# Summing the second router's modulation inside the time mix, and filling the spare expert rows at the start

## The chip, the cores and the metric

The kernel runs on one core of a Trainium2 chip. A core has five engines that follow their own instruction streams and meet at semaphores: TensorE (PE, matrix products), VectorE (DVE), ScalarE (ACT), GpSimd (POOL) and SyncE (SP, which here only issues transfers). The time is device microseconds of one launch of the whole program; the figure of a kernel is the median of its runs.

## The reference

It is a network of two layers on 512 tokens of width 1024, all in float32. What matters here is how the modulation vectors enter:

```python
c_act = jax.nn.silu(c)
for layer in range(2):
    shift, scale, gate = _ada(c_act, ada_w[layer, 0], ada_b[layer, 0])   # c_act @ w + b, split in 3
    h = _rmsnorm(x) * (1 + scale) + shift
    y = even_mixer(h) if layer == 0 else rwkv7_time_mix(h)
    x = x + gate * y
    shift, scale, gate = _ada(c_act, ada_w[layer, 1], ada_b[layer, 1])
    h = _rmsnorm(x) * (1 + scale) + shift
    x = x + gate * moe(h)                # router, two of 16 experts for each token
return _rmsnorm(x) * final_norm_g
```

Each of the four modulations is one vector of 1024 times a 1024 x 3072 matrix, which is 12 MB of weights. They depend on c alone, so they can be worked out anywhere ahead of their use. The last of the four (index 3 in the kernel) belongs to the mixture of experts of layer 1 and is first needed there. The time mix computes three wide projections (v, r and k, each 1024 x 1024) and several narrow ones (w, a, g) of six mixtures of the tokens with their predecessors, and then a recurrence.

## The kernel before

The program is one block with a stream for each engine, in this order of stages: the front (load x, norm, modulation 0), the five projections of layer 0 (q, k, v, u, z), attention and spatial gating, the output product (`out_proj(0, 5)`) with the router's logits in it, the routing and the experts of layer 0 (`moe(0)`), the time mix (`rwkv()`: projections, scan, output product) and the experts of layer 1 (`moe(1)`). Every order is written out by hand. PSUM banks are handed out by `bank_plan`, which lists the uses in PE's order; six banks rotate in ring "a", and the use of a bank waits until the one six places before it is drained.

**A modulation** takes three steps. SP loads 24 pieces of 512 KB (`ada(L, m)` of the sync stream, L610) into a ring of four buffers, `aring`; the load of a piece waits until DVE is done with the piece four before it. DVE multiplies each piece with its column of c and adds it to `acc` (L1205 for the first of a third, L1207 for the rest), one 128x1024 operation for a piece. Then PE sums over the partitions: `mod(k)` is 24 matmuls with a 128x128 block of `acc` as the weights and a single column of ones (L1698). The trace records each float32 matmul as two, so this is "x48". Last, DVE adds the bias (L1213, L1217). `mod(0)` and `mod(1)` make modulation 0 (16 and 8 matmuls), and `mod(2)`, `mod(3)`, `mod(4)` make modulations 1, 2 and 3. Where they stand: `mod(2)` between the products u and z, `mod(3)` at the end of attention, `mod(4)` at the start of `moe(0)`, ahead of the product that ranks the tokens (L1873, L1876).

**The ranking product** waits for "chosen", which DVE signals in `route` at L413 after a chain of small operations. DVE's part of `mod(4)` stands later in `route`, ahead of its wait for that product (L427).

**The 24 pieces of modulation 3** are worked on by DVE in layer 0's output product: 8 ahead of `router_weights(0)` and 4 after each of the first four tiles of `residual(0)`. `aring` and `acc` lie in areas 6 and 7 of the arena. The same areas hold `CB`, the gathered expert rows of `moe`, until all sixteen tiles of x are updated ("x_done" 16), and later R1 and K1 of the time mix.

**The expert rows.** The experts write their rows by item into `expert_rows` (`y_dram`) in DRAM, 24 blocks of 128 rows, of which 16 to 24 are used. SP fills the last eight blocks once with finite numbers: 4 MB from areas 3 and 4 (q, k, v, u of the attention), issued at L652 after the last piece of modulation 2. ACT, DVE and POOL wait for it ("rest_out").

**The time mix's projections.** DVE makes six mixtures, m = 0 to 5, in the two buffers XM[0] and XM[1] by turns (8 operations each, L1478). PE uses them in this order: v (m = 0, tiles 7 and 8, L1715, 8 groups), w (m = 1), a (m = 2), two parts of g (m = 3; all four at L1954), r (m = 4, tiles 9 and 10) and k (m = 5, tiles 11 and 12), both at L1723. Before mixture 2 DVE waits for the last group of v, since v reads the same buffer. PE starts the product a as soon as the first chunk of mixture 2 is there. `recurrence_masks` stands on DVE ahead of mixture 1. SP loads tile 9 when the first half of v is done.

Of the kernel before, what the change touches and what calls it, by code (L numbers as in the profile page):

```python
# [46 lines left out]
def bank_plan():  # L47

    plan, count = [], {}

    def add(kind, ring="a"):
        plan.append((kind, count.get(kind, 0), ring))
        count[kind] = count.get(kind, 0) + 1

    def norm():
        for c in range(KC):
            add("xTa" if c % 2 else "xTv")

    add("vec")
    add("vec")  # L60
    norm()
    add("mod")
    for kind in ("q", "k", "v", "u", "z"):
        for _ in range(4):
            add(kind)
        if kind in ("k", "u"):
            add("mod")
    add("swT")
    add("swT")
    for n in range(NPAIR + 3):  # L70
        if n < NPAIR:
            add("score")
            add("score")
        if NB <= n < 2 * NB:
            add("mix")
        if n >= 2 and n - 2 < NPAIR:
            add("pT")
            add("pT")
        if n >= 3 and (n - 3) % PPB == 0:
            add("o", "b")  # L80
        if NB + 2 <= n < 2 * NB + 2:
            add("sT")
        if n >= 3 and (n - 3) % PPB == PPB - 1:
            if n == NPAIR + 2:
                add("mod")
            add("oT")
    for layer in range(2):
        if layer == 1:
            norm()
            rwkv_plan(add)  # L90
        add("gate")
        add("gate")
        add("lbias", "b")
        for _ in range(NB + 2):
            add("y")
        add("xr")
        add("xr")
        add("logit", "b")
        add("y")
        add("xr")  # L100
        add("xr")
        add("y")
        for _ in range(4):
            add("xr")
        add("gate")
        add("gate")
        if layer == 0:
            add("mod")
        add("rank")
        add("list")  # L110
    return plan


def rwkv_plan(add):
    for _ in range(8):
        add("v1")
    add("wl")
    add("al")
    add("gl")
    add("gl")  # L120
    for _ in range(8):
        add("r1")
    for c in range(KC + 1):
        if c < KC:
            add("k1")
            add("zw")
            add("za")
        if c:
            add("nrm")
    for step in scan_steps():  # L130
        kind = step[0]
        if kind == "turn":
            add("bkT", "p")
            add("bkT", "p")
            add("bon", "ry")
        elif kind == "scores":
            add("sc", "fnpf"[step[2]])
            add("sc", "fnpf"[step[2]])
        elif kind in ("R", "U", "Y", "dS"):
            add(kind, "ry" if kind in ("R", "Y") else "us")  # L140
    for _ in range(2 * NB):
        add("g")
    for _ in range(KC):
        add("yT")
# [81 lines left out]
def build(nc, io):  # L226
    ctx = ExitStack()
    with ctx:
# [123 lines left out]
        def route(v, link, layer, M, mod):  # L352
# [65 lines left out]
            link(nc.vector.reciprocal(su, su))  # L418
            tt(W12[:, 0, :], s1, su, ALU.mult)
            link(tt(W12[:, 1, :], s2, su, ALU.mult))  # L420
            if layer == 0:
                mod(4)

            v.wait_ge(*full("rank", layer + 1))
            ps = bank("rank", layer)
# [161 lines left out]
        def _(sp):  # L587
# [41 lines left out]
            tile(1)  # L629
            for m in range(2 * KC, 3 * KC):  # L630
                ada(0, m)
            sp.dma_start(SW, io["sgu_w"][0].rearrange("g i j -> i g j")).then_inc(sem("sw_in"), 16)
            sp.dma_start(gz, io["sgu_norm_g"][0].partition_broadcast(P)).then_inc(sem("gz_in"), 16)
            sp.dma_start(RWt[:, :, :], io["router_w"].rearrange("(c p) e -> p c e", p=P)).then_inc(sem("rw_in"), 16)
# [10 lines left out]
            tile(6)  # L645
            for m in range(12, 3 * KC):
                ada(2, m)
            sp.wait_ge(*free("u", 4))
            sp.wait_ge(*free("k", 4))
            sp.wait_ge(*free("q", 4))  # L650
            sp.wait_ge(*free("v", 4))
            sp.dma_start(y_dram[NEXP * P:MAX_ITEMS * P, :].rearrange("(k p) f -> p k f", p=P),  # L652
                         arena[:, 3:5, :].rearrange("p a (k f) -> p (a k) f", f=D)).then_inc(sem("rest_out"), 16)
            for m in range(3 * KC):
                ada(3, m)

            def moe(layer):
                M = lambda name: moe_sem(layer, name)
# [73 lines left out]
            sp.wait_ge(sem(f"pair_in{NB - 1}"), 32)  # L732
            tile(7)
            tile(8)
            sp.dma_start(WA2[0:HD, :], io["rwkv_w2"][0]).then_inc(sem("wa2_in"), 16)
            sp.dma_start(WA2[HD:P, :], io["rwkv_a2"][0]).then_inc(sem("wa2_in"), 16)
            for n in range(9, 13):
# [23 lines left out]
        def _(gp):  # L761
# [64 lines left out]
            def moe(layer):  # L826
# [22 lines left out]
                    gp.reg_add(gathered, gathered, 16)  # L849
                    gp.indirect_dma_start(Xg, None, xn_dram, src).then_inc(M("xg_in"), 16)  # L850

                gp.wait_ge(sem("rest_out"), 16)
                gp.wait_ge(M("row_out"), n * 16 + 16)
                gp.reg_add(gathered, gathered, 16)
                gp.wait_ge(M("rows_out"), 16)
# [72 lines left out]
        def _(act):  # L928
# [89 lines left out]
            def moe(layer):  # L1018
# [18 lines left out]
                                                    bias=MOD[:, L, c:c + 1], scale=MOD[:, L, 8 + c:9 + c])  # L1037
                    last.then_inc(M("xga"), 1)

                act.wait_ge(sem("rest_out"), 16)  # L1040
                turned(1)
                act.wait_ge(M("up"), 1)
                act.wait_ge(M("hid"), 1)
# [136 lines left out]
        def _(v):  # L1180
# [74 lines left out]
            def after(layer, n):  # L1255
                if n == 2:
                    v.wait_ge(*full("lbias", layer + 1))
                    nc.vector.tensor_copy(LB[:, :], bank("lbias", layer)[:, 0:NEXP]).then_inc(drained["lbias"], 1)
                if n == 3:
                    diag(2 * layer + 1, 2 * layer + 1)  # L1260
                if n >= NB:
                    v.wait_ge(sem("rest_out"), 16)
                    for half in range(2):
                        k = 8 * layer + 2 * (n - NB) + half
                        v.wait_ge(*full("xr", k + 1))
                        nc.vector.tensor_copy(XR[:, n % 2, 4 * half:4 * half + 4, :],
                                              bank("xr", k).rearrange("p (c t) -> p c t", c=4)
                                              ).then_inc(drained["xr"], 1)

            def residual(layer, more=None):  # L1270

                v.wait_ge(*free("gate", 2 * (2 * layer + 1)))
                for n in range(8):
                    half, b = n // 4, n % 4
                    k = 8 * layer + n
                    v.wait_ge(*full("y", k + 1))
                    cols = slice(half * 512, half * 512 + 512)
                    tt(tmp[:, n % 2, :], bank("y", k), GB[:, cols], ALU.mult).then_inc(drained["y"], 1)
                    v.wait_ge(*free("y", k + 1))
                    tt(X[:, b, cols], X[:, b, cols], tmp[:, n % 2, :], ALU.add).then_inc(sem("x_done"), 1)  # L1280
                    if more:
                        more(n)
                    after(layer, n)

            masks(v, link)
# [85 lines left out]
            del todo[0:8]  # L1371
            diag(0, 0)
            mod(3)
            some_ada(8)
            router_weights(0)
            residual(0, lambda n: some_ada(4 if n < 4 else 0))

            def moe(layer):
                M = lambda name: moe_sem(layer, name)
# [78 lines left out]
            def rwkv():  # L1458
# [9 lines left out]
                for m, mu in enumerate((3, 1, 4, 5, 0, 2)):  # L1468
                    if m == 1:
                        recurrence_masks()  # L1470
                    if m in used:
                        k, n = used[m]
                        v.wait_ge(*full(k, n))
# [204 lines left out]
        def _(pe):  # L1678
# [186 lines left out]
            def moe(layer):  # L1865
                M = lambda name: moe_sem(layer, name)
                L = 2 * layer + 1
                if layer == 0:
                    mod(4)
                out = open_bank(pe, "rank", layer)  # L1870
                pe.wait_ge(sem("chosen"), layer + 1)
                pe.wait_ge(sem("consts"), 9)
# [67 lines left out]
            def rwkv():  # L1940
# [17 lines left out]
                small("al", 0, open_bank(pe, "al", 0)[HD:P, :], A1L, XM[0], 2)  # L1958
                small("gl", 0, open_bank(pe, "gl", 0), G1L[:, :, 0:P], XM[1], 3)
                small("gl", 1, open_bank(pe, "gl", 1)[0:32, :], G1L[:, :, P:P + 32], XM[1], 3)  # L1960
                pe.wait_ge(sem("mixed"), 40)
                for k in range(8):
                    if k % 4 == 0:
# [205 lines left out]
```

## Time and profile before

| | |
|---|---|
| median of 3 runs | 1554.78 us (1553.16 to 1559.13) |
| the profiled execution | 1548.98 us |
| its span | 1547.0 us |
| PE busy | 1336.6 us, 86% |
| DVE busy | 671.6 us, 43% |
| ACT busy | 357.6 us, 23% |
| POOL busy | 254.8 us, 16% |

The span is what the profiler sees from the first to the last instruction; 1.98 us of the profiled execution lie outside it. PE is busy most of the time, but the share is a mean over stages with different limits. So what an edit is worth is read from its own stage: who works there without a pause, and which wait ends last.

### The profile page before, as it was taken

The numbers are of one execution on the slowest core, as the hardware profiler recorded it, in microseconds if no ns is written. First come the engines' busy times: TensorE is split into PE (matmuls) and PEld (weight loads), VectorE is DVE, ScalarE is ACT, GpSimd is POOL, SyncE is SP. The second block draws the span as 40 slices with busy tenths as digits, with TensorE's granted clock in tenths as the row PEclk, the third lists the DMA queues.
The fourth block names the chain that finished last, engine by engine and source line by source line (L and its number), as shares of the span: only waits on it lengthen the run. The fifth ranks groups of instructions, "written<-read, shape, count | busy, mean of one in ns | idle before, by whom it ended". The sixth has DMA issues, their size and how long they took to land.

```text
span 1547.0 us, 23213 instructions
## 1 busy us (share of the span) xinstructions
PE 1336.6 (86%) x8816; PEld 811.9 (52%) x8816; DVE 671.6 (43%) x1373; ACT 357.6 (23%) x806; POOL 254.8 (16%) x263
## 2 busy tenths in 40 slices
PE   0899979997799994699999799999999895999990
PEld 0444557756344441343443688888887454444440
DVE  6426434564133233805026556666763324232324
ACT  1100035102111111101048433333332102211111
POOL 1000037000010012100001423444431200100102
PEclk9999867897899997799999899999997997899995
DMA  8649655373599995311110000000001313699975
GB/s 312 205 143 353 205 191 191 129 252 118 183 348 372 355 355 207 127 55 55 55 54 1 29 3 3 19 2 3 3 2 48 116 55 123 206 344 350 372 274 203
DMA packets 128997, 248.35 MB, mean 161 GB/s; under 512 B 8352, under 2 KB 78192, under 8 KB 128912
## 3 DMA queue, kind: packets, MB, share of 16 engines
q1 hardware_dynamic: 116816, 203.09, 37.9%
q0 software_dynamic: 7344, 26.74, 4.7%
q10 hardware_dynamic: 4752, 17.30, 2.7%
q8 instruction: 63, 1.03, 0.3%
q14 instruction: 22, 0.18, 0.0%
HBM read 219.33 MB, written 27.79 MB: 160 GB/s over the span
## 4 chain that ended last, share of the span: by engine, by line
PE 81%; DVE 8%; issue 4%; DMA 3%; ACT 2%; POOL 1%; POOLq 0%; DVEq 0%; SPq 0%; ACTq 0%
PE PS L1905 15%; PE PS L1723 11%; PE PS L1715 9%; PE PS L1922 7%; PE PS L1767 7%; PE PS L2049 2%; PE PS L2065 2%; PE PS L1894 2%; PE PS L2019 2%; PE PS L2071 2%; PE PS L1698 2%; PE PS L1954 2%; DMA arena<-in_ada_w 2%; PE PS L2104 1%; PE PS L1839 1%
## 5 line engine op out<-in xcount | busy, mean ns | idle before, releaser
L1905 PE MATMUL PS<-WR,arena 128*128 (+1 forms) x528 | 238.8, 606 | 11.3 <-ACT arena L1036 6.2
L1723 PE MATMUL PS<-arena,WR 128*128 128x512 f32 x384 | 168.0, 597 | 3.4 <-ACT arena L970 3.4
L1905 PEld LDWEIGHTS PS<-WR,arena 128*128 128x128 f32 x528 | 99.7, 194 | 128.5 <-issue 124.3
L1715 PE MATMUL PS<-WR,arena 128*128 128x512 f32 x320 | 143.1, 607 | 3.8 <-DVE arena L1478 3.8
L1723 PEld LDWEIGHTS PS<-arena,WR 128*128 128x128 f32 x384 | 73.3, 192 | 96.4 <-issue 92.8
L1922 PE MATMUL PS<-W,arena 128*128 x264 | 119.0, 593 | 3.9 <-DVE arena L1412 3.9
L1207 DVE SCALAR_TENSOR_TENSOR arena<-arena,cact 128x1024 f32<-128x1024 f32 x77 | 98.8, 1283 | 36.5 <-DMA arena<-in_ada_w 31.8
L1767 PE MATMUL PS<-WR,arena 128*128 128x512 f32 x256 | 112.2, 595 | 0.0
L1401 DVE TENSOR_TENSOR arena<-arena,PS 128x256 f32<-128x256 f32 x33 | 13.9, 421 | 212.1 <-ACT arena L1049 191.1
L1715 PEld LDWEIGHTS PS<-WR,arena 128*128 128x128 f32 x320 | 61.6, 195 | 83.2 <-issue 76.3
L796 POOL TENSOR_TENSOR LO<-GB,tmp 128x256 f32<-128x256 f32 x80 | 71.0, 906 | 100.6 <-DVE GB L1540 72.6
L1767 PEld LDWEIGHTS PS<-WR,arena 128*128 128x128 f32 x256 | 48.2, 192 | 56.7 <-issue 56.7
L1049 ACT ACTIVATE arena<-PS 128x256 f32<-128x256 f32 x31 | 11.9, 385 | 284.2 <-PE PS L1905 284.2
L1922 PEld LDWEIGHTS PS<-W,arena 128*128 128x128 f32 x264 | 47.6, 190 | 51.7 <-issue 51.7
L1036 ACT ACTIVATE arena<-PS,MOD 128x128 f32<-128x128 f32 x140 | 52.7, 457 | 62.8 <-PE PS L1894 62.8
L803 POOL TENSOR_TENSOR rstd<-ms,mhalf 128x4 f32<-128x4 f32 x6 | 6.2, 1035 | 355.2 <-DVE ms L1224 355.2
L938 ACT ACTIVATE arena<-arena 128x1024 f32<-128x1024 f32 x20 | 21.1, 1054 | 185.2 <-DVE arena L1280 121.0
L1689 PE MATMUL PS<-ident,arena 128*128 128x128 f32 x64 | 11.0, 353 | 59.6 <-DVE arena L1229 59.6
L1060 ACT ACTIVATE arena<-PS 128x128 f32<-128x128 f32 (+1 forms) x56 | 22.5, 418 | 161.9 <-PE PS L1715 56.8
L850 POOL DMA_INDIRECT arena<-xn_rows,IDX x33 | 31.9, 965 | 160.6 <-PE PS L1894 160.6
L1388 DVE TENSOR_SCALAR arena<-PS,MOD 128x128 f32<-128x128 f32 x140 | 47.8, 404 | 19.6 <-PE PS L1894 18.3
L2049 PE MATMUL PS<-arena,LO 64*64 64x64 f32 x1280 | 48.4, 222 | 8.7 <-ACT arena L1109 5.0
(321 smaller groups left out, 2062.3 us busy)
## 6 DMA issues: line engine op xcount, KB each, us to landing
WR<-in_moe_w SPq DMA_DIRECT2D x66, 1024.0 KB, 7.5
arena<-in_ada_w SPq DMA_DIRECT2D x96, 512.0 KB, 5.2
W<-in_moe_w SPq DMA_DIRECT2D x33, 1024.0 KB
expert_rows<-arena ACTq DMA_DIRECT2D x33, 512.0 KB, 7.2
WR<-in_rwkv_w_rkv SPq DMA_DIRECT2D x6, 2048.0 KB, 7.9
WR<-in_mix_w_in SPq DMA_DIRECT2D x5, 2048.0 KB, 10.6
WR<-in_mix_w_out SPq DMA_DIRECT2D x2, 2048.0 KB, 8.1
expert_rows<-arena SPq DMA_DIRECT2D x1, 4096.0 KB, 14.3
```

What stands on the lines that cost most here:

```text
L796: gp.tensor_tensor(v4(LMc[k % 2]), v4(LTc), JM[:, lv, :].unsqueeze(1).unsqueeze(1).to_broadcast([P, 2, 2, HH]), ALU.mult).then_inc(sem("lm ...
L850: gp.indirect_dma_start(Xg, None, xn_dram, src).then_inc(M("xg_in"), 16)
L1036: last = nc.scalar.activation(XgT[:, c, :], PS[:, 0, c * P:(c + 1) * P], ACT.Identity, bias=MOD[:, L, c:c + 1], scale=MOD[:, L, 8 + c:9 + c])
L1207: stt(a, aring[:, n % 4, :], cact[:, c:c + 1], a, ALU.mult, ALU.add).then_inc(sem("ada_step"), 1)
L1388: last = ts(XgT[:, c, :], PS[:, 1, (c - 4) * P:(c - 3) * P], MOD[:, L, 8 + c:9 + c], MOD[:, L, c:c + 1], ALU.mult, ALU.add)
L1698: last = mm(out[:, j:j + 1], acc[:, j * P:(j + 1) * P], ones[:, 0:1], start=True, stop=True)
L1715: last = mm(out, act_T[:, c, b * P:(b + 1) * P], WR[:, tile % 2, c, :], start=(c == 0), stop=(c == KC - 1))
L1723: last = mm(out, WR[:, tile % 2, c, f * P:(f + 1) * P], act_T[:, c, :], start=(c == 0), stop=(c == KC - 1))
L1767: last = mm(out, HT[:, c, b * P:(b + 1) * P], WR[:, (first_tile + half) % 2, c, :], start=(c == 0), stop=(c == KC - 1))
L1905: last = mm(PS[:, 2, :], XgT[:, c, :], WR[:, slot, c, :].rearrange("p s f -> p (s f)"), start=(c == 0), stop=(c == KC - 1))
L1922: last = mm(PS[:, 6 + half, :], hidT[:, c, :], W2[:, slot, c, half * 512:half * 512 + 512].rearrange("p s f -> p (s f)"), start=(c == 0), ...
L2049: last = mm(XB[g][r, h, j % 2, :], LMc[k % 2][r, h, j, :], Tnc[r, h, j, :], start=True, stop=True)
```

## The change

Four things are moved and none is dropped. `mod(4)` goes on PE from the start of `moe(0)` to the time mix, between the second part of g and the product r; its bank in the plan goes with it. DVE's 24 pieces of modulation 3 leave the output product of layer 0, and stand in one run ahead of mixture 2, before the wait for v; DVE's part of `mod(4)` stands ahead of mixture 5. SP's 24 loads go behind tiles 7 and 8 and a wait for "x_done" 16, ahead of the loads of WA2 (weights of the narrow second products of w and a) and of tile 9. The spare expert rows are filled with two writes of x (2 MB each) in the front, behind the last piece of modulation 0 and ahead of sgu_w, the pieces of modulation 1 and tile 2; the waits of SP for the attention's buffers and of ACT for the write go away, and DVE now waits for it once, ahead of its first change of x.

```diff
@@ bank_plan, rwkv_plan
-        if layer == 0:
-            add("mod")
         add("rank")
...
     add("gl")
     add("gl")
+    add("mod")
@@ route (DVE)
-            if layer == 0:
-                mod(4)
@@ SP
             for m in range(2 * KC, 3 * KC):
                 ada(0, m)
+            for k in (NEXP, NEXP + NB):
+                sp.dma_start(y_dram[k * P:(k + NB) * P, :].rearrange("(b p) f -> p b f", p=P), X
+                             ).then_inc(sem("rest_out"), 16)
...
-            sp.wait_ge(*free("u", 4))
-            sp.wait_ge(*free("k", 4))
-            sp.wait_ge(*free("q", 4))
-            sp.wait_ge(*free("v", 4))
-            sp.dma_start(y_dram[NEXP * P:MAX_ITEMS * P, :].rearrange("(k p) f -> p k f", p=P),
-                         arena[:, 3:5, :].rearrange("p a (k f) -> p (a k) f", f=D)).then_inc(sem("rest_out"), 16)
-            for m in range(3 * KC):
-                ada(3, m)
...
             tile(7)
             tile(8)
+            sp.wait_ge(sem("x_done"), 16)
+            for m in range(3 * KC):
+                ada(3, m)
@@ POOL
-                gp.wait_ge(sem("rest_out"), 16)
+                gp.wait_ge(sem("rest_out"), 32)
@@ ACT, moe
-                act.wait_ge(sem("rest_out"), 16)
@@ DVE, after, residual
-                    v.wait_ge(sem("rest_out"), 16)
...
+                    if n == 0 and layer == 0:
+                        v.wait_ge(sem("rest_out"), 32)
...
-                    if more:
-                        more(n)
@@ DVE, front
-            some_ada(8)
             router_weights(0)
-            residual(0, lambda n: some_ada(4 if n < 4 else 0))
+            residual(0)
@@ DVE, rwkv
                     if m == 1:
                         recurrence_masks()
+                    if m == 2:
+                        some_ada(3 * KC)
+                    if m == 5:
+                        mod(4)
@@ PE, moe
-                if layer == 0:
-                    mod(4)
@@ PE, rwkv
                 small("gl", 1, open_bank(pe, "gl", 1)[0:32, :], G1L[:, :, P:P + 32], XM[1], 3)
+                mod(4)
                 pe.wait_ge(sem("mixed"), 40)
```

## Rows read from the trace of the kernel before

**Rows 1.** The page: span, and the chain's share by engine.

```profile
span 1547.0 us, 23213 instructions
PE 81%; DVE 8%; issue 4%; DMA 3%; ACT 2%; POOL 1%; POOLq 0%; DVEq 0%; SPq 0%; ACTq 0%
```

**Rows 2.** Windows, the output product of layer 0: busy of PE, PEld, DVE, ACT, POOL; PE clock; DMA.

```profile
300.00:350.00 50.00, 50.00 (x154) 25.08 (x153) 35.58 (x47) 2.30 (x4) 0.00 (x0) 1.00 0.75 251
```

**Rows 3.** Chain in order of time, routing of layer 0, then of layer 1: start, us, what.

```profile
364.33 7.30 PE PS L1698 x48
372.27 1.61 PE PS L1876 x8
...
1289.78 7.26 issue
1297.72 1.61 PE PS L1876 x8
```

**Rows 4.** Timeline around the ranking product, layer 0, then layer 1: start, us, engine, what.

```profile
371.26 0.22 DVE L413 TENSOR_TENSOR LO<-LO 128x64 f32<-128x64 f32 x1
371.58 0.68 PE L1873 MATMUL PS<-CHX,upper 128*128 128x80 f32 x2
...
1296.71 0.22 DVE L413 TENSOR_TENSOR LO<-LO 128x64 f32<-128x64 f32 x1
1297.04 0.68 PE L1873 MATMUL PS<-CHX,upper 128*128 128x80 f32 x2 [7.26 <-issue]
```

**Rows 5.** Chain in order of time, time mix from w to r.

```profile
696.66 26.27 PE PS L1954 x64
722.93 62.00 PE PS L1723 x144
```

**Rows 6.** Chain in order of time, around mod(1) and mod(2).

```profile
107.12 1.68 PE PS L1698 x16
...
163.84 7.94 PE PS L1698 x48
171.78 29.87 PE PS L1715 x64
```

**Rows 7.** Windows over mod(2), mod(3) and mod(4), columns as in Rows 2.

```profile
163.68:171.78 8.10, 8.10 (x50) 8.10 (x48) 0.00 (x0) 0.60 (x1) 0.00 (x0) 0.64 0.74 259
...
281.07:290.51 9.44, 9.44 (x51) 9.44 (x51) 2.26 (x9) 0.00 (x0) 0.00 (x0) 0.55 0.00 0
364.18:371.63 7.45, 7.45 (x51) 7.43 (x50) 6.21 (x26) 4.79 (x6) 0.00 (x0) 0.72 0.43 151
```

**Rows 8.** Chain in order of time, first and third up product of layer 0's experts.

```profile
395.58 10.07 PE PS L1905 x16
...
420.15 6.87 PE PS L1905 x16
```

**Rows 9.** Timeline of DVE, mixtures 1 to 4 of the time mix.

```profile
653.26 5.38 DVE L1478 SCALAR_TENSOR_TENSOR arena<-arena,vecB 128x512 f32<-128x512 f32 x8
696.70 5.39 DVE L1478 SCALAR_TENSOR_TENSOR arena<-arena,vecB 128x512 f32<-128x512 f32 x8 [38.06 <-PE PS L1715]
703.71 10.69 DVE L1478 SCALAR_TENSOR_TENSOR arena<-arena,vecB 128x512 f32<-128x512 f32 x16 [1.62 <-PE PS L1954]
```

**Rows 10.** Timeline of DVE, modulation 1: first, sixth and twelfth of twelve pieces.

```profile
109.15 0.75 DVE L1205 TENSOR_SCALAR arena<-arena,cact 128x1024 f32<-128x1024 f32 x1
...
115.76 2.70 DVE L1207 SCALAR_TENSOR_TENSOR arena<-arena,cact 128x1024 f32<-128x1024 f32 x2 [0.27 <-DMA arena<-in_ada_w]
...
125.68 1.28 DVE L1207 SCALAR_TENSOR_TENSOR arena<-arena,cact 128x1024 f32<-128x1024 f32 x1 [0.67 <-DMA arena<-in_ada_w]
```

**Rows 11.** The page: issues of one kind, count, KB each, median us from issue to landing.

```profile
expert_rows<-arena SPq DMA_DIRECT2D x1, 4096.0 KB, 14.3
```

**Rows 12.** Timeline of SP: sgu_w and tile 2 in the front.

```profile
69.63 0.44 SPq L632 DMA_DIRECT2D arena<-in_sgu_w  x1
...
83.36 0.43 SPq L620 DMA_DIRECT2D WR<-in_mix_w_in  x1
```

More of the change, by code:

```diff
@@ L1268, in after, with residual @@
                                               ).then_inc(drained["xr"], 1)
-            def residual(layer, more=None):
+            def residual(layer):
                 v.wait_ge(*free("gate", 2 * (2 * layer + 1)))
```

## The prediction

> **What bounds the kernel now.** I read the page first. PE holds 81% of the chain that ended last, of a span of 1547.0 us [rows 1]. So the first question for every edit is whether PE stands idle where something is taken away, and whether it is busy where something is put. The windows of layer 0's output product show PE busy for 50.00 of 50 us at full clock, while DVE has 35.58 us of work [rows 2]: DVE is not what sets the pace there. Then I read the chain in order of time at the two places that PE's `mod(4)` leaves and enters. At the old place the chain shows it for 7.30 us, as if it were on the path [rows 3]. The timeline says otherwise, and the reader should look at this one closely: the ranking product starts at 371.58 us, and the DVE operation that signals "chosen" (L413) ends at 371.26 + 0.22 = 371.48 us [rows 4]. Two things were ready at nearly one moment. Layer 1 has no `mod(4)`, and there PE waits 7.26 us in the same place, starts 0.11 us behind the end of L413 (1296.93 to 1297.04; layer 0: 0.10), and the time from the last logit product to L1876 is 372.27 - 364.33 = 7.94 us in layer 0 and 1297.72 - 1289.78 = 7.94 us in layer 1 [rows 3, 4]. At the new place PE goes from the narrow products to r at 722.93 us and on without a pause [rows 5].
>
> **The change part by part.**
>
> PE's `mod(4)` taken out of the routing: gain nothing, by the twin in layer 1. It hides behind the 7.15 us that DVE needs from 364.33 to 371.48 [rows 3, 4]. If the sums take longer than this in some executions, the ranking product is late by the difference: the slowest sums of this size took 9.44 us by the windows [rows 7], so the bounds of this term are 0 and 9.44 - 7.15 = 2.3 us gained. I take 0, since the profiled execution is the one that I sum. DVE's two small operations of `mod(4)` also cost nothing here: they stand in front of a wait for the ranking product.
>
> PE's `mod(4)` put between g and r: all of it is on the path, since PE has no idle time on either side [rows 5] and r needs the engine. Its nearest row is `mod(2)`, which also stands between two wide products: 7.94 us [rows 6]. That is more than three times `mod(1)`, which has a third of the matmuls and takes 1.68 us: 5.04 us would be the size at full clock [rows 6]. The windows show why: over `mod(2)` the granted clock is 0.64, over `mod(3)` 0.55 and over `mod(4)` 0.72, with PE busy all the time [rows 7]. A half is 1.2 GHz and 1.00 is 2.4 GHz, so the clock falls in the course of the sums, at another moment each time, and the three took 8.10, 9.44 and 7.45 us by the windows.
>
> The clock does not come back at once. The product z behind `mod(2)` has 64 recorded matmuls and takes 29.87 us [rows 6]; at the rate of r and k's clean run, 62.00 / 144 = 0.431 us, it would take 27.56 [rows 5]. So 2.3 us more are lost. For comparison, the first up product of the experts, which starts on an engine that stood idle, takes 10.07 us where the third takes 6.87: 3.2 us [rows 8]. This term lies between 0 (clock at full) and 3.2; I take 2.3, from the place that is like the new one. In front of the sums there is nothing to add: the trace gives the narrow products 26.27 us for 64, and they stay as they are.
>
> New cost: 7.94 + 2.3 = 10.2 us. Low end with a fall of the clock: 7.45 + 1.6, half the largest loss behind it, about 9.1; high end 9.44 + 3.2 = 12.6; without any fall 5.04.
>
> The Trainium skill ("TensorE: Matmul & The Clock Gate", Part 1: The HAM clock gate) says that the clock is set by how busy the engine has been lately, and that the engine runs at 2.4 GHz while it is busy. Taken at its word the rule keeps the clock up, since PE's queue is full of work, and gives 5.04 us in place of 10.2. The trace does not bear it out for this kind of matmul: three out of three runs of 24 fell.
>
> DVE's 24 pieces taken out of the output product: gain nothing, since PE never pauses there [rows 2]. The same for their 12 MB and the 4 MB write on SP's queue: the experts' first weights go out earlier, but the first up product starts at 395.58 us [rows 8] behind the routing, not behind a load.
>
> DVE's 24 pieces put ahead of mixture 2: DVE is free from 653.26 + 5.38 = 658.6 us until 696.70, a gap of 38.06 us that ends with the last group of v [rows 9]. Twelve pieces of modulation 1, with four in the ring at the start as here, took from 109.15 to 125.68 + 1.28 = 126.96, 17.8 us; the last seven of them went at 11.2 / 7 = 1.60 us each [rows 10]. So 24 take 17.8 + 12 x 1.60 = 37.0 us and end at 695.6, just inside the gap. As a bound from above take the rate of the 4 MB write, 14.3 us for eight times 512 KB [rows 11], that is 1.79 us each: 43.0 us, end at 701.6. That is late for mixture 2 but not for PE, which works on w until about 703.6 (mixture 3 waits until 703.71 for it [rows 9]). Mixture 2 is then made chunk by chunk at 5.39 / 8 = 0.67 us, faster than PE's 26.27 / 32 = 0.82 us for a chunk [rows 5], so only its first chunk must be there, and DVE must begin by 703.6 - 0.7 = 702.9. The price is 0 in both cases, and it begins at (702.9 - 658.6) / 24 = 1.85 us a piece. Behind DVE in this stretch only mixtures 2 to 5 are queued, and only PE's a waits for them.
>
> SP's queue: the loads of WA2 and tiles 9 and 10 stand behind the last piece, so behind DVE's 20th, about 689 us. Tile 9 is due at 722.93 plus the sums. One tile is 2 MB, 7.2 us at the write's rate [rows 11]: in time by far. Tile 7 is ahead of the pieces.
>
> The two writes of x in the front: SP's row at 69.63 is where they go out; tile 2 follows at 83.36 [rows 12]. Queued by then are 4 MB of writes, 2 MB of pieces, 0.8 MB of small loads and the 2 MB tile: 8.8 MB at 3.5 us a MB is 31 us, so the tile lands at 100.5, and PE needs it at 107.12 + 1.68 = 108.8 [rows 6, 11, 12]. Slack 8 us, price 0. DVE's new wait for the writes ends two hundred microseconds before it is reached.
>
> PSUM: r's sixth group now waits for DVE to drain the bank of the sums, which DVE does as soon as they end, five groups ahead. Price 0.
>
> Sum: 0 + 10.2 + 0. The profiled execution of 1548.98 us would become 1559.2 and its span 1557.2. That execution is 5.8 us below the median of the runs shown; the same 10.2 us on 1554.78 give 1565.0.
>
> **The rivals.**
>
> *The clock stays up* (the other side, no longer slower by more than can be told). The narrow products ahead are dense, and if the sums ran at 2.4 GHz they would cost 5.04 us and nothing behind them: 1559.8, or 0.32%. For it: the sums of `mod(1)` did run at full clock [rows 6]. Against it: they are a third as long, and all three long ones fell, two of them behind equally dense work [rows 7]. It decides when fall and aftermath together cost under 2.8 us, since 0.5% is 7.8 us.
>
> *The pieces come late.* At 2.0 us a piece DVE starts mixture 2 at 706.6 instead of 702.9 and PE stands for 3.7 us, which also cools it: 14 us or more, 1569 and up. For it: the spare time is 1 us by the best estimate of the end of v, and 7 us by PE's need. Against it: behind tiles 7 and 8 SP issues nothing else until DVE is at its 20th piece.
>
> *Tile 2 comes late in the front.* Each microsecond of landing behind 108.8 costs one. If writes to DRAM slow the queue by half again, 46 us, the tile lands at 129 and the cost is 20 us on top: 1585. Against it: the one write of this kind shows no such rate.
>
> *The sums were in the way after all.* If in most executions `mod(4)` outlasts DVE's chain, up to 2.3 us come back: 1562.7. By itself it never makes the kernel faster.
>
> **How the numbers follow.** Clock falls, pieces and tile in time, with up to 2.3 us given back: 0.78. Clock stays up: 0.09. Pieces or tile late: 0.09. Something on the other side that I have not seen, such as less traffic beside the output product: 0.04. The likeliest gives 1565.0. Its own bounds are 9.1 - 2.3 = 6.8 and 12.6 us, 1561.6 to 1567.4; with 3 us for the spread of medians and the case of the high clock the range is 1558.8 to 1570. A difference of 0.5% (7.8 us) is about what a measurement of this kernel can tell from no change. Slower: 0.8 of the likeliest case and all the late ones, 0.71. Same: the rest of the likeliest, the high clock and half of the last, 0.26. Faster: 0.03.
>
> **What the changed profile would show.** L1698 x48 stands in the chain between L1954 and L1723 with some 8 us, granted clock 0.55 to 0.72 over it, and the start of r at half clock. In the routing of layer 0 an idle of about 7.2 us replaces the sums, and L1876 still starts 7.9 us behind the last logit product. DVE's run of L1207 goes from 658.6 to about 696 and PE goes from w to a without a gap. PE at 108.8 does not wait for tile 2. The prediction is wrong if the clock holds at 2.4 GHz through the sums, if a gap stands ahead of a or the product v of layer 0, or if L1876 comes nearer to the logits.

## The result, and the profile after

The changed kernel takes 1558.47 us (median of 18 runs, 1549.68 to 1569.88), and the kernel before 1551.89 us (median of 18, the three shown ahead among them). The ratio is 1.0051, with a 95% interval of 1.0029 to 1.0073: slower by 7.9 us, between 4.5 and 11.3. Put on the 1554.78 us that the prediction started from, this is 1562.7 us. The prediction was 1565.0 and slower by 10.2 us, with bounds of 6.8 to 12.6 for the likeliest case.

The profiled execution took 1555.13 us. The page of the changed kernel, its span and the chain's share by engine:

```profile
span 1553.1 us, 23203 instructions
PE 81%; DVE 8%; issue 4%; DMA 3%; ACT 2%; POOL 2%; POOLq 0%; DVEq 0%; SPq 0%; ACTq 0%
```

In the shares the change does not show. The chain in order of time shows it at the new place, where before the w, a and g products and r followed on each other [rows 5]:

```profile
695.85 26.27 PE PS L1948 x64
722.12 8.42 PE PS L1694 x48
730.54 63.90 PE PS L1719 x144
```

The sums take 8.42 us, and r's first 144 records 63.90 where they took 62.00. Together that is 10.32 us more, against 10.2 in the prediction. The windows over the sums and over the start of r (busy of PE, PEld, DVE, ACT, POOL, the granted clock, DMA) show why:

```profile
722.05:730.54 8.49, 8.49 (x50) 8.49 (x49) 0.00 (x0) 0.59 (x1) 0.00 (x0) 0.63 0.01 2
730.54:733.00 2.46, 2.46 (x3) 1.01 (x4) 2.39 (x6) 0.00 (x0) 0.00 (x0) 0.50 0.00 0
733.00:734.00 1.00, 1.00 (x3) 0.39 (x2) 1.00 (x2) 0.00 (x0) 0.00 (x0) 0.50 0.00 0
734.00:735.00 1.00, 1.00 (x3) 0.48 (x2) 1.00 (x3) 0.00 (x0) 0.00 (x0) 0.79 0.00 0
735.00:736.00 1.00, 1.00 (x4) 0.48 (x3) 1.00 (x2) 0.00 (x0) 0.00 (x0) 1.00 0.00 0
```

PE is busy throughout, yet the clock falls during the sums (mean 0.63) and r begins at 0.50, which is 1.2 GHz; 2.4 GHz is back within the stretch from 734 us, and from 735 us on it is 1.00.

At the old place the chain holds an idle stretch of the same length as the sums that stood there [rows 3]:

```profile
366.06 7.26 issue
373.32 0.69 PE PS L1867 x2
374.01 1.61 PE PS L1870 x8
```

L1870, which was L1876, starts 374.01 - 366.06 = 7.95 us behind the last logit product; it was 7.94. Nothing was gained there in these two executions. On DVE, the last two pieces of modulation 3 and the mixtures 2 to 4 (timeline of DVE, changed kernel):

```profile
692.53 1.28 DVE L1201 SCALAR_TENSOR_TENSOR arena<-arena,cact 128x1024 f32<-128x1024 f32 x1 [0.78 <-DMA arena<-in_ada_w]
696.00 1.28 DVE L1201 SCALAR_TENSOR_TENSOR arena<-arena,cact 128x1024 f32<-128x1024 f32 x1 [2.18 <-DMA arena<-in_ada_w]
697.20 5.38 DVE L1474 SCALAR_TENSOR_TENSOR arena<-arena,vecB 128x512 f32<-128x512 f32 x8
702.90 10.69 DVE L1474 SCALAR_TENSOR_TENSOR arena<-arena,vecB 128x512 f32<-128x512 f32 x16 [0.32 <-PE PS L1948]
```

The pieces begin at 657.75 and end at 697.28, 39.5 us instead of the 37.0 of the prediction. Mixture 2 starts 1.35 us behind the end of v (695.85), and PE does not notice: the chain has no gap ahead of or inside L1948.

### The profile page after: what moved, and what is told of

It reads as the page before. It is cut to its first block, busy times and chain, and to the rows that moved or that the text cites. A ratio compares the mean times of both kernels' runs of the same rounds, so it can differ in the third digit from the quotient of the medians.

```text
span 1553.1 us, 23203 instructions
## 1 busy us (share of the span) xinstructions
PE 1336.6 (86%) x8816; PEld 810.1 (52%) x8816; DVE 672.0 (43%) x1373; ACT 357.2 (23%) x806; POOL 254.3 (16%) x263
## 4 chain that ended last, share of the span: by engine, by line
PE 81%; DVE 8%; issue 4%; DMA 3%; ACT 2%; POOL 2%; POOLq 0%; DVEq 0%; SPq 0%; ACTq 0%
PE PS L1899 15%; PE PS L1719 11%; PE PS L1711 9%; PE PS L1916 7%; PE PS L1763 7%; PE PS L2044 2%; PE PS L2060 2%; PE PS L1888 2%; PE PS L2014 2%; PE PS L2066 2%; PE PS L1694 2%; PE PS L1948 2%; DMA arena<-in_ada_w 1%; PE PS L2099 1%; PE PS L1835 1%
## 5 line engine op out<-in xcount | busy, mean ns | idle before, releaser
L1719 PE MATMUL PS<-arena,WR 128*128 128x512 f32 x384 | 171.6, 607 | 3.4 <-ACT arena L965 3.4
L1399 DVE TENSOR_TENSOR arena<-PS,GB 128x512 f32<-128x512 f32 x33 | 22.8, 692 | 75.5 <-PE PS L1916 75.5
## 6 DMA issues: line engine op xcount, KB each, us to landing
WR<-in_rwkv_w_rkv SPq DMA_DIRECT2D x6, 2048.0 KB, 10.3
```

Source lines behind the costliest of these rows:

```text
L1719: last = mm(out, WR[:, tile % 2, c, f * P:(f + 1) * P], act_T[:, c, :], start=(c == 0), stop=(c == KC - 1))
```

## The experiments

Each kernel was timed against the kernel before on the same chip, but for experiments 8 and 9, which are one profiled execution each. Two figures are given: the ratio of whole times, whose interval is 0.2 to 0.35% to each side (3 to 5 us), and the stage's own length in the profile. The stage length is from the end of g to the end of r's first 144 records, which is 62.00 us in the kernel before. The stage length comes from one profiled execution of each kernel.

### 1. The fill alone in the front

```diff
+            for k in (NEXP, NEXP + NB):
+                sp.dma_start(y_dram[k * P:(k + NB) * P, :].rearrange("(b p) f -> p b f", p=P), X
+                             ).then_inc(sem("rest_out"), 16)
             sp.dma_start(SW, io["sgu_w"][0].rearrange("g i j -> i g j")).then_inc(sem("sw_in"), 16)
...
-            sp.dma_start(y_dram[NEXP * P:MAX_ITEMS * P, :].rearrange("(k p) f -> p k f", p=P),
-                         arena[:, 3:5, :].rearrange("p a (k f) -> p (a k) f", f=D)).then_inc(sem("rest_out"), 16)
```

> The kernel before, with one edit: the spare expert rows are filled by the two writes of x in the front instead of by the one write after attention. My theory (the fill costs and gives nothing): 0 us, within 0.3% of before; in the profile tile 2 lands before PE asks for it, no gap on PE ahead of the product v. Rival (the queue is choked in the front): PE waits for tile 2 and the kernel is slower by the length of that gap. Second rival (the write after attention was in somebody's way, and this is what the whole change gets back): faster by 2 to 3 us, with a wait in attention or in the output product that is gone.

Measured: 1550.44 us against 1551.02, ratio 0.9995 (0.9975 to 1.0016). So the fill costs less than 3 us, and the likeliest value is nothing. A gain of 2 to 3 us, the second rival, is not seen, but the interval (3.9 us faster to 2.5 us slower) does not exclude it. But it is not as quiet in the front as I had it. In the timeline of SP's issues in this kernel, the issue of the small load of the norm's weights (L636), behind the two writes, takes 10.26 us in place of 1.11, and tile 2 goes out later:

```profile
69.94 0.98 SPq L633 DMA_DIRECT2D expert_rows<-arena  x2
...
72.50 10.26 SPq L636 DMA_DIRECT2D arena<-in_sgu_norm_g  x1
...
87.55 0.66 SPq L620 DMA_DIRECT2D WR<-in_mix_w_in  x1
```

Tile 2 goes out at 87.55 instead of 83.36 us [rows 12], and the slowest tile of this tensor needed 16.3 us to land. That is 103.9 at the latest, and PE asks for it at 109.1. PE is busy for 8.00 of the 8 us from 104 to 112 us, so it does not wait. The price is still 0, with 5 us to spare and not 8.

### 2. The sums alone at the new place

```diff
+                spare = open_bank(pe, "r1", 0)
+                for j in range(24):
+                    mm(spare[:, j:j + 1], acc[:, j * P:(j + 1) * P], ones[:, 0:1], start=True, stop=True)
                 pe.wait_ge(sem("mixed"), 40)
```

> The kernel before, with 24 more one-column matmuls at the new place (between g and r), which sum whatever stands in acc and whose result is overwritten; nothing is moved. My theory: these sums alone are the whole cost of the change, 8 to 9.4 us for themselves and 2 to 3 us of half clock at the start of r, 10.2 us in all, ratio 1.0065. Rival (clock stays up): 5.0 us, ratio 1.0033. Rival (the move of the pieces and the queues costs something too): this kernel costs clearly less than the whole change does in its stage.

Measured: 1562.75 us against 1551.02, ratio 1.0092 (1.0058 to 1.0126). In the profile of this kernel, chain in order of time, the block was cheaper than in the changed kernel:

```profile
718.31 5.45 PE PS L1963 x48
723.76 63.60 PE PS L1723 x144
```

That is 5.45 + 1.60 = 7.05 us, and the windows tell how it comes about:

```profile
718.31:723.76 5.45, 5.45 (x50) 5.45 (x50) 5.39 (x8) 0.59 (x1) 0.00 (x0) 1.00 0.00 0
723.76:727.00 3.24, 3.24 (x4) 1.26 (x5) 0.00 (x0) 0.00 (x0) 0.00 (x0) 0.50 0.00 0
```

The clock held through all the sums and fell just behind them, so that only r paid. So "the clock stays up" happens for the block itself, but the drop then comes in r. The cost of the block is not one number. The whole program slowed by 9 to 20 us, more than this profile explains; the profiled execution was the shortest of this kernel's (1547.44 us, of 1547.44 to 1572.26). What the stage costs is read from the profiles, what the kernel costs from the ratios. The ratio supports that the sums alone bring the slowdown. Its lower end, 9 us, lies above the 5.0 of the rival, but experiment 4 will show a ratio that also lies above its own stage, so the stage is the stronger evidence: 7.05 us in this profile, and a clock that fell.

### 3. The sums back in the routing, beside the changed kernel

```diff
                 out = open_bank(pe, "rank", layer)
+                if layer == 0:
+                    for j in range(24):
+                        mm(out[:, 400 + j:401 + j], acc[:, j * P:(j + 1) * P], ones[:, 0:1], start=True, stop=True)
                 pe.wait_ge(sem("chosen"), layer + 1)
```

> The kernel after, with an idle set of the same 24 matmuls put back into the routing of layer 0, ahead of the wait for chosen; the result is not used. My theory: same time as the kernel after, since DVE's chain of 7.15 us covers them; at most 2.3 us more in executions in which the clock falls early. If the mean is near 2 us more, then the sums were partly in the way in the routing, and that is what the change gets back of its 10.2 us. In the profile: L1876's counterpart starts 7.9 us behind the last logit product if they are covered, later if not.

Measured: 1559.32 us against 1551.02, ratio 1.0065 (1.0043 to 1.0087). The changed kernel has 1.0051 (1.0029 to 1.0073), so the difference is +0.14% with an interval of some 0.3% to each side: no cost that can be told, and 2 us neither shown nor excluded by the times. The timeline of this kernel (L412 signals "chosen" here) shows the two within a hair:

```profile
365.39 0.22 DVE L412 TENSOR_TENSOR LO<-LO 128x64 f32<-128x64 f32 x1
365.76 0.69 PE L1870 MATMUL PS<-CHX,upper 128*128 128x80 f32 x2
```

The start is 0.15 us behind the signal, where it was 0.10 and 0.11 [rows 4]. In the profile of experiment 2, whose routing is that of the kernel before, it is 0.55 us (signal 366.38 + 0.22, start 367.15), since there the sums took 7.84 us. The largest value is in the profile of experiment 10, where they took 8.31 us (L415 signals "chosen" there):

```profile
366.22 0.22 DVE L415 TENSOR_TENSOR LO<-LO 128x64 f32<-128x64 f32 x1
367.45 0.69 PE L1888 MATMUL PS<-CHX,upper 128*128 128x80 f32 x2
```

The product starts 1.01 us behind the signal, so 0.9 us were lost. In the other four profiles with the sums in the routing (before, 1, 4 and 12) it is 0.09 to 0.11. So the sums in the routing cost 0.0 to 0.9 us in the seven executions seen, 0.2 in the mean, and never the 2.3 of the bound.

### 4. Wide matmuls in place of the thin ones

```diff
+                spare = open_bank(pe, "r1", 0)
+                for j in range(6):
+                    mm(spare, ones[:, :], acc[:, j * 512:(j + 1) * 512], start=True, stop=True)
                 pe.wait_ge(sem("mixed"), 40)
```

> The kernel before, with 6 matmuls of 512 columns (ones as weights, acc as the moving side) at the new place instead of 24 of one column; the result is overwritten. It covers the same 3072 columns of acc. At full clock both sets take about 5.2 us by the rows. My theory (half of the cost is the clock, which thin matmuls let fall): about 5.2 us, granted clock 1.00 throughout, r takes 62.0 us as before; ratio 1.0033. Rival (the cost is the number of records or the weights, not the clock): less than 3 us. Rival (the clock falls at this place whatever is put there): 8 us or more.

Measured: 1560.12 us against 1551.02, ratio 1.0055 (1.0034 to 1.0075). Chain and windows of this kernel, stage by stage:

```profile
725.75 5.35 PE PS L1963 x12
731.10 61.80 PE PS L1723 x144
```

```profile
725.75:731.10 5.35, 5.35 (x14) 2.48 (x14) 5.31 (x8) 0.59 (x1) 0.00 (x0) 1.00 0.00 0
731.10:792.90 61.80, 61.80 (x147) 27.08 (x145) 0.08 (x1) 4.78 (x8) 0.00 (x0) 1.00 0.19 67
```

The stage takes 67.15 us, 5.15 more than before, at full clock from end to end. So the place does not bring the clock down, the thin matmuls do. What it is about them that lets it fall, the number of columns or the change of weights with each matmul, is not separated here. The ratio, 5.3 to 11.6 us, lies a little above the stage's 5.15, and the profiled span is 13.7 us longer than before (1560.7 against 1547.0); the other 8.5 us lie outside the stage, and their cause is open. By the whole times, thin and wide (1.0092 and 1.0055) differ by 0.37% with an interval of some 0.4% to each side: the difference between them is shown by stage and clock, not by the ratios.

### 5 and 6. The sums between r's matmuls

```diff
+                def between(n):
+                    for j in range(each * n, each * n + each):
+                        if j < 24:
+                            last = mm(sums[:, j:j + 1], acc[:, j * P:(j + 1) * P], ones[:, 0:1], start=True, stop=True)
...
-                mod(4)
...
                 for c in range(KC):
+                    if between:
+                        between(KC * k + c)
                     last = mm(out, WR[:, tile % 2, c, f * P:(f + 1) * P], act_T[:, c, :], start=(c == 0),
```

`each` stands for 1 in experiment 5, one sum for each of 24 matmuls, and 3 in experiment 6, three for each of the first eight.

> The kernel after, with the 24 sums of mod(4) set one by one in front of the first 24 of r's wide matmuls instead of in a block ahead of them. My theory (the sums cost their own 5.0 to 5.5 us at full clock, and everything above it is the clock that a block of thin matmuls lets fall): the granted clock is 1.00 over the whole of r, and from the end of g to the end of r's first 144 records it takes 62.0 + 5.0 = 67 us where the kernel after took 72.3; ratio to before about 1.0033. Rival (the clock falls whatever stands between them): 70 us or more.

> As the last one, but three sums in front of each of r's first 8 matmuls, so a denser mixture. My theory: also 67 us, clock 1.00, if a wide matmul now and then is enough to keep the clock; a rival is that the share of thin matmuls is already too high here, and the clock falls as in the block: 69 us or more.

Measured: 1555.42 and 1556.13 us against 1550.08, ratios 1.0034 (1.0007 to 1.0060) and 1.0045 (1.0020 to 1.0070). The windows over the stage, first of the one with one sum for each matmul, then of the one with three:

```profile
717.58:784.94 67.36, 67.36 (x194) 32.65 (x194) 5.64 (x10) 5.36 (x9) 0.00 (x0) 1.00 0.17 62
```

```profile
717.11:784.46 67.35, 67.35 (x194) 32.63 (x194) 5.64 (x10) 5.36 (x9) 0.00 (x0) 1.00 0.17 62
```

The stages take 5.36 and 5.35 us more than 62.00, at clock 1.00, whatever the mixture. This is the same work as in the block of the changed kernel, which cost 10.32 us in its profile. So there 5.35 us was the work and 4.97 us the clock. The ratios agree with 5.35 us, but by themselves they do not tell these kernels from the changed one (1.0051).

### 7. All but the fill: sums, pieces and loads

The kernel after with the old fill (the first hunk of experiment 1 undone).

> The kernel after with the old fill of the spare expert rows (one write of 4 MB from areas 3 and 4 after attention), so of the change only the sums, the pieces and their loads are moved. My theory: the same time as the kernel after, ratio about 1.005 to 1.006, since the fill alone measured 0.9995. Rival (the fill in the front costs something that only shows together with the rest): nearer to before than the kernel after is.

Measured: 1562.40 us against 1551.62, ratio 1.0072 (1.0043 to 1.0100). It does not differ from the changed kernel beyond the intervals, and it is clearly slower than before. The slowdown sits in this part; a cost or gain of the fill below some 3 us is not excluded. Its stage is 8.04 + 2.29 = 10.33 us longer (8.04 for the sums, 64.29 for r).

### 8. The pieces held back

```diff
             sp.wait_ge(sem("x_done"), 16)
+            sp.wait_ge(*full("v1", 3))
             for m in range(3 * KC):
                 ada(3, m)
```

> The kernel after, with SP's loads of the 24 pieces held back until the third group of v is done (about 662 us) instead of until x is updated (623 us). It tests the margin that I gave this step. My theory: the first piece lands at about 668, 24 pieces at 1.6 us end near 706, DVE starts mixture 2 there instead of at 697, and PE, which needs its first chunk at about 703, stands for 3 to 4 us ahead of a; less than 39 us of delay comes through. Rival (PE waits for all of mixture 2, or the loads are slower beside tile 9): 8 us or more of gap.

One profiled execution. The first piece is worked on at 666.57, the last ends at 705.70, and mixture 2 starts at 705.62. PE has one gap, ahead of a (timeline of PE in this kernel):

```profile
697.01 7.08 PE L1949 MATMUL PS<-arena,LO 128*64 128x512 f32 x16
706.51 21.10 PE L1949 MATMUL PS<-arena,LO 128*64 128x512 f32 x48 [2.42 <-DVE arena L1475]
```

The loads went out 39.8 us later (662.83 against 623.06), but DVE, which in the changed kernel was not free for them before 657.75, began only 8.8 us later, and 2.42 us came through to PE. That is a little less than the 3 to 4 us that I expected. By the working of the prediction the deadline here is the end of w less one chunk, 697.01 + 7.08 - 0.7 = 703.4 us. Mixture 2 missed it by 2.2 us, and PE's gap is 2.42. The rival's 8 us are excluded.

### 9. The changed kernel once more

> The kernel after once more, unchanged, for one more profile of the same program. My theory: the cost of the block of thin matmuls (sums and the excess of r's first 144 records over 62.0 us) is not a fixed 10.3 us but falls anywhere between 7 and 12 us by the moment at which the clock drops; so this value should differ from 10.32 us. Rival (it is fixed by the place): 10.3 us again.

One profiled execution. The chain gives, for the same program:

```profile
725.48 7.82 PE PS L1694 x48
733.30 64.52 PE PS L1719 x144
```

That is 7.82 + 2.52 = 10.34 us. The parts differ from the first profile (8.42 and 1.90), the sum does not. My expectation of any value between 7 and 12 was wrong for this pair. Over all profiles with the thin block at this place the cost is 10.32, 10.34, 10.33 (experiment 7), 7.05 (experiment 2), 5.49 + 1.56 = 7.05 (experiment 3) and 6.23 + 2.48 = 8.71 us (experiment 8). So these six took one of three values, 1.6 us apart, and their mean is 9.0.

### 10. mod(2) spread in the kernel before

```diff
-                    rows(kind, b, b, 2 + n, HT)
-                if kind == "u":
-                    mod(2)
+                    rows(kind, b, b, 2 + n, HT, between=spread(2) if (kind, b) == ("u", 3) else None)
```

`spread(k)` puts three of the 24 sums in front of each of a group's eight matmuls.

> The kernel before with mod(2) alone spread over the last group of u. The block cost 10.3 us in five of the profiles so far and 8.7 us in three (sums and the excess of z together), the spread form 5.35 us. My theory: 3.4 to 5.0 us or 0.2 to 0.3% faster than before, which is half of what spreading mod(2) and mod(3) together gave. Rival (all of that gain came from mod(3)): no difference.

Measured: 1546.61 us against 1551.62, ratio 0.9961 (0.9938 to 0.9984): faster by 6.0 us, between 2.5 and 9.6, which agrees with the 3.4 to 5.0 expected. From the start of v to the end of z the kernel before takes 201.65 - 108.80 = 92.85 us [rows 6], and this one 168.43 + 28.45 - 109.00 = 87.88, so 4.97 us less.

### 11 and 12. All large sums spread, on the changed kernel and on the one before

On the changed kernel: `mod(2)` as in 10, `mod(3)` in the first group of layer 0's output product, `mod(4)` as in 6. On the kernel before: `mod(2)` and `mod(3)` in the same way, `mod(4)` left in the routing, and DVE's 24 pieces placed behind the tiles of the output product.

```diff
-            mod(3)
-            some_ada(8)
             router_weights(0)
-            residual(0, lambda n: some_ada(4 if n < 4 else 0))
+            mod(3)
+            residual(0, lambda n: some_ada((5, 5, 4, 4, 2, 2, 2, 0)[n]))
...
+                        between = spread(3) if k == 0 else None
```

> The kernel after, with all three large sums spread three by three: mod(2) in the last group of u, mod(3) in the first group of layer 0's output product (possible since the change keeps acc free there), mod(4) in the first group of r. My theory: each saves what the half clock cost, in the profile of before 7.94 + 2.3 - 5.0 = 5.2 us for mod(2), some 5 us for mod(3) (its 9.27 less 5.0, the slow gate product behind it, less about 1.5 us of waits that it covered), and 5 us for mod(4): 15 us less than the kernel after, so 7 us or 0.5% faster than before. Rival (the clock losses are given back at the next stall anyway): no faster than before.

> The kernel before, with mod(2) spread in the last group of u and mod(3) in the first group of the output product; mod(4) stays in the routing, and its 24 pieces on DVE start after the first group and are spread over the first seven tiles of the output product. My theory: 5.2 + 5 us saved and mod(4) still free, 10 us or 0.65% faster than before, if DVE keeps up in the output product. Rival: DVE is late for x and the logits there, PE waits, and 3 us or more come back as gaps in the output product.

Measured: 1549.51 us, ratio 0.9998 (0.9971 to 1.0026), and 1540.87 us, ratio 0.9938 (0.9914 to 0.9961), both against 1550.08. The second is the one to keep: 9.6 us faster than before (6.0 to 13.3), and faster than the changed kernel. Its output product, from the end of attention to the last logit product, takes 358.18 - 278.92 = 79.26 us where the kernel before takes 364.33 - 281.23 = 83.10; with the 4.96 us of `mod(2)` (here 199.59 - 111.70 = 87.89) the two stages give 8.8 us. The chain in its routing, as in [rows 3]:

```profile
358.18 6.94 PE PS L1699 x48
366.12 1.61 PE PS L1891 x8
```

`mod(4)` is still free here, L1891 7.94 us behind the last logit product. DVE kept up: PE is busy for 63.00 of the 63 us from 295 to 358 us.

On the changed kernel I expected 7 us faster than before, and it came out level. My arithmetic was off by 1.6 us in what `mod(3)` gives and by 2.3 in the start, since I took the changed kernel as 8 us slower where its stage says 10.3. By the stages it saves 5.0 us for `mod(2)` and 79.69 against 83.10 = 3.4 for the output product, and it still pays 5.35 for `mod(4)`, which leaves 3.0 us or a ratio of 0.9981, inside the interval.

## Why the prediction was right, point by point

**PE out of the routing, 0 us (bound 2.3).** Held. L1870 stands 7.95 us behind the logits, and putting the sums back (experiment 3) costs nothing that the times show. In the seven profiles with the sums in the routing the ranking product was late by nothing in four, by 0.05 and 0.4 in two, and by 0.9 us in one. So the rival that the sums were in the way after all holds in a small part, 0.2 us in the mean. That the chain named the sums for 7.30 us [rows 3] was no sign that they were in the way; the start of the ranking product against the signal was.

**PE between g and r, 10.2 us.** The mechanism held: the work is on the path, and half of its price is the clock. The term was mis-sized slightly upward. In the profiles of the changed kernel it is 10.32 and 10.34, but the six profiles with this block give 7.05 to 10.34, mean 9.0, and the whole kernel measured 7.9 us (4.5 to 11.3). I took the one value of `mod(2)` that the profile of before happened to show, and that the changed kernel's profile then came within 0.1 us of it is in part luck. The low end with a fall of the clock, 9.1, was wrong: two of the six profiles have 7.05 us and one 8.71, all with a fall. At 7.05 fall and slow start together cost 2.0 us over the 5.04, which by the prediction's own mark of 2.8 us counts for the rival. In the other ten profiles with this block at `mod(2)`'s place the same sum (block, and z over 27.56) comes to 10.3 in seven and to 8.6 in three, among these the changed kernel's (6.47 + 29.71 - 27.56). The likeliest value was right and a mean would have been lower.

**The clock.** That thin matmuls bring it down is shown by experiments 4 to 6: the same place, the same columns of acc or the very same sums, with wide matmuls or between them, stay at 1.00 and cost 5.15 and 5.35 us. The rule of the Trainium skill ("TensorE: Matmul & The Clock Gate", Part 1: The HAM clock gate), that a busy engine runs at 2.4 GHz, does not hold here if busy is what the profile calls busy: in the block of weight loads and one-column matmuls the windows show PE busy for 8.49 of 8.49 us at a mean of 0.63. The rival built on it, 5.04 us for the block with nothing behind it, is not what any of the six profiles shows: the least is 7.05.

**DVE's pieces, 0 us.** Held, with less to spare than reckoned: they took 39.5 us and not 37.0, since the last pieces landed late (2.18 us of wait for the last). The way in which the deadline of 702.9 us was worked out agrees with the one point behind it (experiment 8). In the changed kernel it is 695.85 + 7.08 - 0.7 = 702.2, and mixture 2 started at 697.20, so 5.0 us remained. The rival "the pieces come late" was not what happened, and its price, one for one from the deadline on, agrees with experiment 8 (2.2 us late, 2.42 us of gap). SP's next loads went out at 688.85 us, as worked out (689).

**The fill, 0 us.** Held (0.9995). The working was too hopeful: SP itself was held up for 10 us at the load behind the writes, and tile 2 had 5 us to spare instead of 8. The price of the rival with the late tile was summed wrongly: the likely case counts its 31 us from 69.63, the rival its 46 us from 83.36. From the same start the tile would land at about 116 and cost 7 us, not 20. Neither came about.

**The sum.** One profiled pair would mislead. The spans differ by 6.1 us, of which the new place gives +10.3. The other 4.2 us come off in stretches where PE has the same work in both kernels, or the moved sums cost nothing: the front is 3.6 us longer up to `mod(1)`, `mod(2)` with z 1.6 us shorter, the stretch from there to the start of v 2.8 us shorter, and all that follows r's 144 records 3.4 us shorter (+3.6 - 1.6 - 2.8 + 10.3 - 3.4 = +6.1). The part in `mod(2)` is the spread just told of. The front is of the same kind: `mod(0)`'s last records take 3.59 us instead of 2.16 at a granted clock of 0.50 instead of 0.87, and the product behind them 58.20 instead of 56.59, together 3.0 of the 3.6 us. It is not the fill: the six profiles without it in the front reach `mod(1)` at 106.4 to 110.4 us (mean 108.4) and the eight with it at 106.5 to 110.7 (mean 108.6), and in both groups the late ones are those in which `mod(0)`'s records take 3.6 us. Of the 2.8 us, 2.5 lie between the last logit product and v, in the routing and the experts of layer 0. There the seven profiles with the sums in the routing take 283.1 to 286.0 us (mean 283.9), and the seven without them 280.6 to 284.2 (mean 282.8). A gain of about 1 us is possible there and would bring the 9.0 us of the block nearer to the 7.9 of the whole, but the two groups overlap and it is not shown. For the last 3.4 us no cause was shown.

## What to carry to other kernels

Before moving work off a stage, compare the start of what follows with the last signal it waited for, or with a twin stage that lacks the work; the chain alone names whichever came last by a hair. A block of 24 one-column float32 matmuls between wide products cost 1.3 to 1.9 times its work here (7.05 to 10.3 us for 5.35), since the clock falls during it or right behind it and comes back late; set them singly or in threes between the wide ones, where they cost their own 5.35 us, or leave them where the engine would idle. And price such a block over several executions, for it does not take the same value in each.

## What was not expected of the hardware

The cost of the thin block, with the slow start of the product behind it, took three values in the six profiles, 7.05, 8.7 and 10.3 us, and none between. Within the largest, where the block itself is shorter, the product behind it is longer by as much (8.42 + 1.90, 7.82 + 2.52 and 8.04 + 2.29 all give 10.3). The smallest came when the clock fell at the very end of the block or behind it (experiments 2 and 3, mean clock over the block 1.00 and 0.98). Three thin matmuls to one wide one keep the clock at 1.00 as well as one to one does (67.35 and 67.36 us). And with two writes of 2 MB in front of it, SP's own issue of a small load took 10.26 us where it took 1.11 before, so that what stands behind it in SP's order went out later. Not all of it adds up: the four loads of pieces behind took 2.13 us to issue instead of 8.44, and from the sgu_w load or the writes (69.63 and 69.94) to tile 2 SP needed 17.6 us instead of 13.7.
